# A two-layer mixer kernel: the gate chunks of both mixers two head steps later, half pairs split early, eight convolution taps moved from GpSimd to VectorE

## What is computed

```python
proj = u @ w_in          # q, k, v (3 x 512), glu_in (2 x 512), g_attn (1024), g_conv (1024)
attn = causal attention of 8 heads of 64 (q and k with partial rope)
h = a * sigmoid(g)                                 # a, g = split(glu_in)
h = causal depthwise convolution(h, 31 taps) + dw_b
h = silu(layer_norm(h, ln_g, ln_b))
merged = sigmoid(g_attn) * (attn @ w_attn_br) + sigmoid(g_conv) * (h @ w_conv_pw)
return merged @ w_out
```

## Time and profile before

| | |
|---|---|
| median of three runs | 1989.61 us (1987.58 to 1997.01) |
| the profiled execution | 1984.26 us, of which its span is 1982.5 us |
| TensorE matmul, busy | 1840.3 us, 93% |
| VectorE, busy | 1406.2 us, 71% |
| ScalarE, busy | 956.4 us, 48% |
| GpSimd, busy | 829.4 us, 42% |
| mean granted TensorE clock | 0.959 of full speed |
| mixer mix0, attention's first scores to the first matmul of chunk 18 | 1233.39 to 1303.97 us |
| mixer mix1, the same | 1636.19 to 1707.22 us |

### The profile page before, as it was taken

How to read it: one execution, slowest core, us unless ns; L and a number is a source line. 1 busy time by engine, 2 the same in 40 slices (tenths; PEclk the granted TensorE clock), 3 DMA queues, 4 the chain that set the end, 5 groups by cost and what they waited for, 6 DMA issues and landing times.

```text
span 1982.5 us, 28192 instructions
## 1 busy us (share of the span) xinstructions
PE 1840.3 (93%) x11324; PEld 1624.9 (82%) x11324; DVE 1406.2 (71%) x1502; ACT 956.4 (48%) x1182; POOL 829.4 (42%) x392
## 2 busy tenths in 40 slices
PE   7999999999999999988899979988999899889997
PEld 6788798788888888867788869978888798878886
DVE  6987554499858995565988559856864489668643
ACT  5454453445434543445454342855543447555432
POOL 5967200097649766020976829900000069400000
PEclk9999997899999999999999978999999899999998
DMA  7777442366775876632587644334655344336550
GB/s 236 247 247 246 157 150 85 106 223 225 251 243 194 259 239 208 190 101 96 181 258 241 206 137 140 108 115 131 191 191 178 125 152 144 112 107 193 189 190 23
DMA packets 346549, 347.75 MB, mean 175 GB/s; under 512 B 15124, under 2 KB 341576, under 8 KB 346440
## 3 DMA queue, kind: packets, MB, share of 16 engines
q1 hardware_dynamic: 346408, 346.18, 53.9%
q10 hardware_dynamic: 32, 0.02, 0.0%
HBM read 345.11 MB, written 1.07 MB: 175 GB/s over the span
## 4 chain that ended last, share of the span: by engine, by line
PE 43%; issue 31%; POOL 12%; DVE 10%; ACT 3%; DMA 1%; POOLq 1%; SPq 0%; DVEq 0%; ACTq 0%
PE bank L861 19%; PE bank L860 10%; POOL arena L783 4%; POOL arena L749 4%; DVE wl L1734 3%; POOL arena L746 3%; PE bank L804 3%; PE bank L805 2%; PE bank L806 2%; DVE hx L1799 1%; PE bank L849 1%; ACT wh L1330 1%; DVE xn L1765 1%; PE bank L1228 1%; PE bank L1031 1%
## 5 line engine op out<-in xcount | busy, mean ns | idle before, releaser
L1734 DVE TENSOR_TENSOR wl<-raw,wh 128x2048 fp32r<-128x2048 f32 (+1 forms) x279 | 749.3, 2686 | 327.6 <-ACT wh L1330 327.3
L861 PE MATMUL bank<-xx,wh 128*128 128x512 f32 x1920 | 682.0, 399 | 0.0
L1330 ACT ACTIVATE wh<-raw 128x2048 fp32r<-128x2048 f32 (+1 forms) x279 | 525.9, 1885 | 251.6 <-PE bank L861 193.1
L860 PE MATMUL bank<-xx,wl 128*128 128x256 f32 x1920 | 544.8, 284 | 45.1 <-DVE arena L1790 22.0
L861 PEld LDWEIGHTS bank<-xx,wh 128*128 128x128 f32 x1920 | 365.3, 190 | 84.9
L861 PE MATMUL bank<-hx,wh 128*128 128x512 f32 x1216 | 427.7, 395 | 0.0
L860 PEld LDWEIGHTS bank<-xx,wl 128*128 128x128 f32 x1920 | 367.9, 192 | 53.4 <-issue 47.9
L746 POOL TENSOR_TENSOR arena<-arena,csil 128x2048 f32<-128x2048 f32 x48 | 223.1, 4647 | 394.7 <-DVE xx L1745 206.7
L804 PE MATMUL bank<-xx,wh 128*128 128x256 f32 x1136 | 333.4, 293 | 29.1 <-DVE xx L2084 15.3
L860 PE MATMUL bank<-hx,wl 128*128 128x256 f32 x1216 | 344.9, 284 | 0.0
L805 PE MATMUL bank<-xx,wh 128*128 128x256 f32 x1136 | 327.6, 288 | 0.0
(11 more groups left out here) (278 smaller groups left out, 1887.2 us busy)
## 6 DMA issues: line engine op xcount, KB each, us to landing
raw<-in_ffn_w_in SPq DMA_DIRECT2D x88, 1024.0 KB, 5.2
arena<-in_w_ada SPq DMA_DIRECT2D x48, 1024.0 KB, 7.8
raw<-in_w_in SPq DMA_DIRECT2D x36, 1024.0 KB, 4.9
raw<-in_ffn_w_out SPq DMA_DIRECT2D x32, 1024.0 KB, 5.7
raw<-in_w_up SPq DMA_DIRECT2D x32, 1024.0 KB, 5.4
raw<-in_w_down SPq DMA_DIRECT2D x32, 1024.0 KB, 5.1
raw<-in_ffn_w_out SPq DMA_DIRECT2D x16, 768.0 KB, 6.7
raw<-in_even_w_in SPq DMA_DIRECT2D x12, 1024.0 KB, 5.3
```

The lines of the kernel that those rows point to most:

```text
L860: pe.matmul(o[:, 0:T], lo_w, halves[:, 0, :], start=start, stop=False, skip_group_check=True)
L861: return pe.matmul(o.rearrange("p (h t) -> p h t", h=2), hi_w, halves, start=False, stop=stop, skip_group_check=True)
L1330: act.activation(wh[:, c % RING, at], raw[:, c % RING, at], ACT.Copy).then_inc(hi_made.sem, 1)
L1734: dve.tensor_tensor(wl[:, c % RING, at], raw[:, c % RING, at], wh[:, c % RING, at].bitcast(F32), ALU.subtract).then_inc(lo_made.sem, 1)
```

## The change

Four edits, in both mixers.

1. **Gate chunks.** `GATES_FROM = 2`: chunk 10 + i - 2 instead of 10 + i is done in step i, on TensorE and ScalarE, and `lo` of the matching chunk two steps later on VectorE. Steps 0 and 1 have no chunk, steps 8 and 9 have one.
2. **Taps.** GpSimd does taps 0 to 22 of its two tiles (`POOL_TAPS = 23`), so 22 pairs of a product and an addition instead of 30. Taps 23 to 30 of tiles 2 and 3 are 16 operations appended to VectorE's list of taps, behind its own 62, in place in `cacc`; the first waits until GpSimd's part is done. TensorE waits for VectorE's last tap alone.
3. **Halves.** ScalarE copies pairs 0 to 2 of `ao` to `xh` in step 9 of the loop, ahead of the last pair's `upper`, and pair 3 after the loop; VectorE makes `xl` in two pieces as well.
4. **Mean.** The copy of the mean to `cmu` on ScalarE goes; VectorE subtracts it in one operation that reads it from PSUM.

```diff
+POOL_TAPS = 23
+    GATES_FROM = 2
-    per_conv = 2 + 2 * (CONV_K - 1)
+    per_conv = 2 + 2 * (POOL_TAPS - 1)
 # pool_mix
-            with pool.Fori(0, (CONV_K - 1) // 2) as g:
+            with pool.Fori(0, (POOL_TAPS - 1) // 2) as g:
 # pe_mix
-            pe_attention(s, lambda i: pe_chunk(s, 10 + i, c0 + 10 + i, False) if i < 8 else None)
+            def gates(i):
+                n = 10 + i - GATES_FROM
+                if 10 <= n < 18:
+                    pe_chunk(s, n, c0 + n, False)
+            pe_attention(s, gates)
             pe.wait_ge(conv_made.sem, conv_made.at(s))
-            pe.wait_ge(pool_step.sem, pool_conv[s])
...
-                    pe.wait_ge(cln_act.sem, cln_act.at(s, 2))
+                    pe.wait_ge(cln_act.sem, cln_act.at(s, 1))
...
-                pe.wait_ge(xl_made.sem, xl_made.at(s, 1 if n < 2 else 3))
+                pe.wait_ge(xl_made.sem, xl_made.at(s, 2 if n < 2 else 4))
 # act_attention, behind evacuate(i - 2)
+                if KIND[s] == "mix" and i == H + 1:
+                    act.wait_ge(ao_made.sem, ao_made.at(s, 3))
+                    act.activation(xh[:, 0:3, :], ao[:, 0:3, :], ACT.Copy).then_inc(xh_made.sem, 1)
 # act_mix (gates(i) as in pe_mix)
-            act.activation(xh[:, 0:4, :], ao, ACT.Copy).then_inc(xh_made.sem, 1)
-            act.wait_ge(cln_pe.sem, cln_pe.at(s, 1))
-            act.activation(cmu, bank[6][:, 0:T], ACT.Copy, scale=1.0 / CW).then_inc(cln_act.sem, 1)
+            act.activation(xh[:, 3, :], ao[:, 3, :], ACT.Copy).then_inc(xh_made.sem, 1)
 # dve_mix
-            taps = [(j, ct) for j in range(CONV_K) for ct in range(2)]
+            taps = [(j, ct) for j in range(CONV_K) for ct in range(2)] + [(j, ct) for j in range(POOL_TAPS, CONV_K) for ct in (2, 3)]
...
+                    if ct >= 2:
+                        n = CONV_K * 2 + (j - POOL_TAPS) * 2 + ct - 2
+                        if j == POOL_TAPS:
+                            dve.wait_ge(pool_step.sem, pool_conv[s])
+                        else:
+                            dve.wait_ge(conv_made.sem, conv_made.at(s, n - 1))
+                        dve.scalar_tensor_tensor(out=cacc[:, ct, :], in0=src, scalar=w, in1=cacc[:, ct, :], op0=ALU.mult,
+                                                 op1=ALU.add).then_inc(conv_made.sem, 1)
+                        continue
...
-                if 1 <= i <= 8:
-                    lo(c0 + 9 + i + RING)
+                n = 10 + i - GATES_FROM - 1
+                if 10 <= n < 18:
+                    lo(c0 + n + RING)
...
-            dve.wait_ge(xh_made.sem, xh_made.at(s, 1))
-            dve.tensor_tensor(xl[:, 0:4, :], ao, xh[:, 0:4, :].bitcast(F32), ALU.subtract).then_inc(xl_made.sem, 1)
-            dve.wait_ge(cln_act.sem, cln_act.at(s, 1))
-            dve.tensor_tensor(cacc, cacc, cmu.unsqueeze(1).broadcast_to((P, CT, T)), ALU.subtract).then_inc(cln_dve.sem, 1)
+            for i, at in enumerate((slice(0, 3), slice(3, 4))):
+                dve.wait_ge(xh_made.sem, xh_made.at(s, i + 1))
+                dve.tensor_tensor(xl[:, at, :], ao[:, at, :], xh[:, at, :].bitcast(F32), ALU.subtract).then_inc(xl_made.sem, 1)
+            dve.wait_ge(cln_pe.sem, cln_pe.at(s, 1))
+            dve.scalar_tensor_tensor(out=cacc, in0=bank[6][:, 0:T].unsqueeze(1).broadcast_to((P, CT, T)), scalar=-1.0 / CW, in1=cacc,
+                                     op0=ALU.mult, op1=ALU.add).then_inc(cln_dve.sem, 1)
```

More of the change, by code:

```diff
@@ L241, in build @@
     yt = c.take(2 * 512, "p (b t) -> p b t", b=2)
-    cmu = c.take(T)
     ptmp = c.take(2 * 2 * T, "p (b c t) -> p b c t", b=2, c=2)
@@ L372, in build @@
             glu_made.plan(s, 1)
-            conv_made.plan(s, CONV_K * 2)
-            for g, n in ((rope_pe, 4), (rope_dve, 4), (ao_made, 4), (cln_pe, 2), (cln_act, 3 + CT), (cln_dve, 1 + CT),
-                         (xh_made, 1 + 2 + 4), (xl_made, 1 + 2 + 4), (merged, 4), (y_out, 4), (x_ready, 4)):
+            conv_made.plan(s, CONV_K * 2 + (CONV_K - POOL_TAPS) * 2)
+            for g, n in ((rope_pe, 4), (rope_dve, 4), (ao_made, 4), (cln_pe, 2), (cln_act, 2 + CT), (cln_dve, 1 + CT),
+                         (xh_made, 2 + 2 + 4), (xl_made, 2 + 2 + 4), (merged, 4), (y_out, 4), (x_ready, 4)):
                 g.plan(s, n)
@@ L935, in ready @@
         def ready(s, k):
-            return {"mix": 3 + 1 + k // 2, "even": 1 + max(0, k - 3), "odd": k + 1}[KIND[s]]
+            return {"mix": 4 + 1 + k // 2, "even": 1 + max(0, k - 3), "odd": k + 1}[KIND[s]]
         def pe_out(s, c0):
@@ L1649, in act_mix, with gates @@
                         act_ln_bias(x_of[s])
-            act_attention(s, lambda i: act_chunk(s, 10 + i, c0 + 10 + i, ACT.Sigmoid, pm) if i < 8 else None)
+            def gates(i):
+                n = 10 + i - GATES_FROM
+                if 10 <= n < 18:
+                    act_chunk(s, n, c0 + n, ACT.Sigmoid, pm)
+            act_attention(s, gates)
             act.wait_ge(ao_made.sem, ao_made.at(s))
-            act.activation(xh[:, 0:4, :], ao, ACT.Copy).then_inc(xh_made.sem, 1)
-            act.wait_ge(cln_pe.sem, cln_pe.at(s, 1))
-            act.activation(cmu, bank[6][:, 0:T], ACT.Copy, scale=1.0 / CW).then_inc(cln_act.sem, 1)
+            act.activation(xh[:, 3, :], ao[:, 3, :], ACT.Copy).then_inc(xh_made.sem, 1)
             act.wait_ge(cln_dve.sem, cln_dve.at(s, 1))
@@ L1663, in act_mix @@
             for q in range(2):
-                act.wait_ge(cln_act.sem, cln_act.at(s, 5 + 2 * q))
+                act.wait_ge(cln_act.sem, cln_act.at(s, 4 + 2 * q))
                 act.activation(xh[:, 4 + 2 * q:6 + 2 * q, :], ctmp[:, 2 * q:2 * q + 2, :], ACT.Copy).then_inc(xh_made.sem, 1)
@@ L2109, in dve_mix @@
                 dve.wait_ge(ada_summed.sem, ada_summed.at("ffn3"))
-            taps = [(j, ct) for j in range(CONV_K) for ct in range(2)]
+            taps = [(j, ct) for j in range(CONV_K) for ct in range(2)] + [(j, ct) for j in range(POOL_TAPS, CONV_K) for ct in (2, 3)]
             def convolve(count):
                 for j, ct in taps[:count]:
+                    w, src = vec(2 + l, j * CT + ct), hpad[:, ct, j:j + T]
+                    if ct >= 2:
[7 more added lines that the diff above has]
+                        continue
                     n = j * 2 + ct
-                    w, src = vec(2 + l, j * CT + ct), hpad[:, ct, j:j + T]
                     acc = bank[1][:, ct * T:(ct + 1) * T]
@@ L2185, in merge @@
                 for i in (2 * n, 2 * n + 1):
-                    dve.wait_ge(xh_made.sem, xh_made.at(s, 3 + i + 1))
+                    dve.wait_ge(xh_made.sem, xh_made.at(s, 4 + i + 1))
                     at = slice(2 * i, 2 * i + 2)
@@ L2190, in dve_mix @@
             link(gate_attention(0))
-            dve.wait_ge(cln_act.sem, cln_act.at(s, 3))
+            dve.wait_ge(cln_act.sem, cln_act.at(s, 2))
             link(dve.reciprocal(rstd[:, :], root[:, :]))
@@ L2196, in dve_mix @@
             for q in range(2):
-                dve.wait_ge(xh_made.sem, xh_made.at(s, 2 + q))
+                dve.wait_ge(xh_made.sem, xh_made.at(s, 3 + q))
                 dve.tensor_tensor(xl[:, 4 + 2 * q:6 + 2 * q, :], ctmp[:, 2 * q:2 * q + 2, :],
```

## The result

The changed kernel takes 1999.8 us (median of nine runs, 1995.76 to 2008.34), the kernel before 1989.61 us (nine runs, 1978.44 to 1998.09). The ratio is 1.0052, with a 95% interval of 1.0033 to 1.0072. So the change costs 0.52%, or 10.3 us, beside a forecast of 11.2 us and 2000.8 us. The profiled execution took 1998.08 us.

The account below looks back on a forecast made before the run. TensorE, busy 93%, was taken to bound the kernel. Mix1 at 78.9 us (+7.9) and mix0 at 73.95 (+3.4) gave +11.2 us on the 1989.6 median, so 2000.8 us, range 1990 to 2008.

Parts of the forecast that it names:

- What bounds: TensorE, 93% busy, bounds both mixers; everything the change can win lies inside 5.3 us of its idle time.
- the two marks: In each mixer, the attention's first scores and chunk 18's first matmul: 71.03 us apart in mix1, 70.58 in mix0.
- the loop's middle: Steps 3 to 7 of the attention loop: same work on every engine, TensorE keeps the pace, nothing gained or lost.
- Front, mix1: Start of mix1's attention: TensorE idles 6.94 us before head 2's scores, plus 1.38 us for scores at the lower clock.
- Front, mix0: Start of mix0's attention: TensorE idles 1.63 us before head 2's scores, plus 1.38 us for slower scores.
- the clock returns sooner: Rival, chunk 10: less time at half clock; all gone leaves +3.6 us, half gives +7.5, about 1997; chance 0.27.
- Tail: Each mixer's end: 1.82 us wait for the transposes' copy in place of 1.27, then 0.8 us for the low halves.
- the clock falls in the tail: Rival, before chunk 18: two idle pieces lower the clock, 1.3 us lost per mixer, +13.8 us, 2003.4; chance 0.12.
- Taps: VectorE, steps 6 to 9: 16 moved taps at 0.472 us, 7.6 us per mixer, hidden by gate chunks, costing nothing.
- The sum: Between first scores and chunk 18: mix1 78.9 us (+7.9), mix0 73.95 (+3.4), together +11.2; chance 0.42 within 1.5 us.
- no front wait: Rival, head 2's scores: masked scores come in time, total -0.1 us, or -1.7 with `lo` out of the way; chance 0.07.
- VectorE becomes the bound: Rival, both mixers: moved taps uncovered or waiting on GpSimd too early, up to 7.6 us more each, 2016; chance 0.05.

Follow-up runs that it names:

- the best version: Changed kernel with gate chunks one step later, eight moved taps, chunk 20's split behind the attention output's splits: 1981.4 us, ratio 0.9958 to before.

## Why the prediction was right

**What bounds.** Right: the change acts on TensorE's idle time between the two marks, and only there; the loop's middle kept its pace. From the end of chunk 10 to the end of chunk 17 mix1 took 1715.49 - 1662.58 = 52.91 us against 52.27, with two steps' transposes and outputs more in it (2.42 us) and two heads' scores less (1.70). VectorE and ScalarE waited for TensorE in it. One bound was too tight: I had put all that can be won inside the 5.3 us of idle time, and the best version is 7.3 us shorter between the marks, in part because the scores of two heads take less time when they stand together.

**Front, mix1.** I worked out 6.94 us of idle time and 1.38 us for slower scores, 8.32 us; the trace has 8.41 us of idle time. The sum was right, its parts were not. Scores of heads 0 and 1 together took 1.66 us, not twice 1.54. Their matmuls run side by side: each head lies on 64 of the 128 partitions, an even head on the lower half and an odd one on the upper (`half(h)`), and the matmuls of the two start within 0.05 us of each other. Two windows of 0.04 us, at the start of heads 0 and 1 and at the start of head 2, which is alone, show two matmuls and one:

```profile
1642.80:1642.84 0.04, 0.02 (x2) 0.04 (x2) 0.04 (x1) 0.04 (x1) 0.04 (x1) 0.50 0.00 0
...
1652.88:1652.92 0.04, 0.03 (x1) 0.03 (x1) 0.04 (x1) 0.04 (x1) 0.04 (x1) 0.50 1.08 384
```

So the second head of a pair costs next to nothing when its scores follow at once, 1.59 us to the chunk behind for two heads in the run with a shift of one, and 1.54 for one head in the earlier trace rows. Head 2's scores took 1654.47 - 1652.89 = 1.58 us. The error did not reach the sum: VectorE's end of the queue came 10.01 us behind the first scores, 10.02 before, and whatever TensorE does not spend on two heads it waits. From first scores to chunk 10 it took 11.65 us, where my terms give 11.56.

**Front, mix0.** The same mistake, 1.63 us of idle time forecast and 3.19 measured, and again it cancels: 6.41 us from first scores to chunk 10, and 6.34 by my terms. Chunk 10 took 1247.38 - 1240.23 = 7.15 us, where I had kept 8.02. Windows of the changed kernel, mix0's chunk 10 first and then mix1's:

```profile
1240.23:1243.40 3.17, 3.17 (x16) 3.17 (x16) 3.13 (x10) 0.99 (x4) 3.09 (x4) 0.53 0.00 0
...
1654.47:1659.50 5.03, 5.03 (x24) 5.03 (x24) 4.96 (x19) 1.69 (x7) 4.87 (x5) 0.50 0.05 15
```

In mix0 the clock came back 3.2 us into the chunk, in mix1 only 5.0 us into it, as before. The rival *the clock returns sooner* was half true, for one mixer.

**Tail.** The wait for the copy: 1.82 us forecast, 1.74 in both mixers. The wait for the low halves: 0.8 forecast. The row of mix1 says 0.45, counted from the modelled end of the sums; from start to start, as in the forecast, it is 1721.76 - 1719.31 - 1.62 = 0.83 us. In mix0 no wait shows. There the sums themselves took 1306.87 - 1304.12 = 2.75 us instead of 1.62:

```profile
1304.10:1308.00 3.90, 3.90 (x13) 3.25 (x13) 2.85 (x4) 0.80 (x2) 0.00 (x0) 0.57 0.33 110
```

The clock had fallen to 0.57, so *the clock falls in the tail* was true in mix0, and not in mix1 with the same wait of 1.74 us (1.00 from 1719.3 to 1722.0). The rule of the Trainium skill (TensorE: Matmul & The Clock Gate, HAM oscillation) that pauses between bursts cost the full rate each time is told there of waits longer than these, and I stretched it to this tail: it agrees with mix0 and does not show in mix1. VectorE had the low halves of mix0 done at 1306.42. In mix1 chunk 18 began 0.14 us behind that point, so at the full clock chunk 18 of mix0 would have begun near 1306.56 and not at 1306.87. By this estimate the lower clock cost 0.3 of its 1.1 us, and the other 0.8 hid the wait.

**Taps.** Sixteen of them at 0.477 us, where I took 0.472. These are the changed kernel's moved taps in mix1, grouped by form (count, busy us, mean ns):

```profile
L2133 DVE SCALAR_TENSOR_TENSOR arena<-arena,vecT 128x256 f32<-128x256 f32 x16 | 6.7, 477 | 0.0
```

No wait at the first: GpSimd's 22nd addition ended at 1679.33 + 1.29 = 1680.62, and VectorE came to its tap behind its own last two, near 1692. Those two rows:

```profile
1679.33 1.29 POOL L786 TENSOR_TENSOR arena<-arena 128x512 f32<-128x512 f32 x1
```

```profile
1691.91 1.27 DVE L2133 SCALAR_TENSOR_TENSOR arena<-arena,vecT 128x256 f32<-128x256 f32 x3
```

The margin was 11 us, where I had put some 3: VectorE came later in step 6 than I had worked out, and GpSimd's end lay 4 us earlier against the first scores than before. The cost of the taps was nothing, and the run with the taps back shows it. I had forecast that an uncovered tap costs; the runs with a shift of none and of one show that the cover was the delay itself: it fails by 2.33 and 1.61 us as soon as the front wait is gone.

**The sum.** Mix1 78.9 forecast and 78.94 measured, mix0 73.95 and 73.05, together +11.2 and +10.4 us; the runs give +10.3. In mix0 errors cancel in part: chunk 10 took 0.87 us less than I kept, the tail behind the last chunk 0.3 us more (1306.87 - 1300.30 = 6.57, where my terms give 6.25), and the 68.32 us of work held 0.37 us of waiting, since the 0.99 of the earlier trace rows is counted from the modelled end of the sums (they start at 1300.99, and 1303.97 - 1300.99 - 1.62 = 1.36). That the forecast median came within 1.0 us is luck beyond what the sum can claim: the interval of the measured ratio is some 4 us wide on either side. The rivals *no front wait* and *VectorE becomes the bound* are refuted, the first by the 8.41 us, the second by the run with the gate chunks alone.

## What to carry to other kernels

Work that stands between two dependent steps on the bounding engine is cover for a third engine's queue; before it is moved, read how far that engine is behind at that point (here 8.4 us in mix1), not only what it does in between. In an order written by hand the last and the first step are special: the last chunk filled nothing, because the copy TensorE waited for stood behind 1.9 us of work wanted 20 us later, and putting that work last brought 3.0 us between the marks of the two mixers together, with a shift of one step, and 2.9 without. And an edit that is free beside a loss has to be costed again without it.

## What was not expected of the hardware

The granted clock took different turns at the same gaps: behind the same wait of 1.74 us it was down during mix0's sums and up during mix1's, in one execution. And the start of mix0's attention, behind stages that are the same, lay up to 13 us apart between executions, more than the whole effect of this change; the lower clock of the later ones goes with it, and how much of it is the clock's is not shown.

VectorE's smallest operations are not always small. One product of 8 elements per partition, in the changed kernel in front of mix0's attention while GpSimd adds and multiplies, and in the run with the fold late, where GpSimd is silent:

```profile
1234.48 1.24 DVE L2083 TENSOR_TENSOR fold<-vecT,adaT 128x8 f32<-128x8 f32 x1
```

```profile
1304.46 0.16 DVE L2083 TENSOR_TENSOR fold<-vecT,adaT 128x8 f32<-128x8 f32 x1
```

All six of them took 3.6 us in the first place and 0.7 in the second; in the first, three of the six were slow (0.96 to 1.24 us) and three were not (0.15 to 0.17). That GpSimd is the reason was not tried by itself.
